# A two-layer hybrid backbone: MLP weights converted by HBM-to-HBM casting DMAs, and the RG-LRU gate loop split in two

## The chip, the cores and the metric

The kernel runs on all 8 cores of one Trainium2 chip. Every core computes one element of the batch with the same program and no exchange between cores. The metric is the device time in microseconds of the slowest core; a lower time is better.

## What is computed

x (8 x 2048 x 1024) and a context of 256 tokens go through two layers. Each layer is: RMSNorm and adaLN modulation, one input projection, three kinds of token mixers, one output projection, a gated residual, then a modulated squared-ReLU MLP (1024 to 4096 to 1024). The part on which the change works is the first kind of mixer, the RG-LRU, in both directions, and the weights of the MLP:

```python
r = jax.nn.sigmoid(gates[0])
i = jax.nn.sigmoid(gates[1])
log_a = -LRU_C * r * jax.nn.softplus(-lam)
a = jnp.exp(log_a)
b = jnp.sqrt(-jnp.expm1(2.0 * log_a)) * (i * xc)
a_cum, h = lax.associative_scan(_lin_combine, (a, b), axis=1)
...
def sq_relu_mlp(h, w1, w2):
    return jnp.square(jax.nn.relu(h @ w1)) @ w2
```

All inputs are float32. The kernel multiplies in bf16, so each weight is converted once or more on its way.

## The kernel before

The tokens of one core (256 of context, then 2048 latent, 2304 in all) lie in SBUF as X, channels on the partitions, float32. CHUNKS cuts the token axis into one chunk of 256 and four of 512. The kernel runs these stages in order: load_x (x through three staging buffers, transposed on TensorE); then per layer ada (48 blocks of ada_w, 512 KB each, through five staging buffers, cast to bf16 in turn by VectorE and ScalarE, one small product each), derive, the norm of all chunks into HT, two small projections (Wl with 16 columns, W24 with 120), the groups, and mlp; at the end final.

The groups of a layer are two RG-LRU groups of 128 channels (group_a), then six pair groups (group_pair: three of linear attention, three of mLSTM). Each group projects HT, gates, scans and adds its part of the output projection to X (finish_group).

group_a loads four weights by wload: a DMA on SP's queue into one of two float32 staging buffers (STG), then a cast on an engine, which is POOL when nothing is said (L408 to L423). Wo takes the place of Wx in SBUF. Then come the projection with Wx, the one with Wg and its gelu, the convolution, and the gate loop (L670 to L693): for each of two directions and each chunk, two products with 128x128 gate matrices, a Sigmoid, two Exp, a Sqrt and a second Sigmoid on ScalarE, two multiplies on VectorE; after the five chunks a scan on VectorE (L369) over all tokens.

The MLP's weights are converted in the background while the RG-LRU groups run. bg_setup makes a list of 64 jobs per layer (32 blocks of w1, 32 of w2); bg(n), called at many places of group_a, takes n of them: SP loads 512 KB of float32, POOL casts, and SP stores 256 KB of bf16 to the HBM scratch w1s or w2s, one job late (bg_flush). All 64 are done within the two RG-LRU groups. mlp then reads w1s and w2s: a first pass over the 256 context tokens (layer 0 only), then two passes over 1024 latent tokens. A pass loads each w1 block once and each w2 block once for every 512 tokens, through six buffers each (wload_cached).

There is no scheduler. The order on each engine is the order in which the code is written; Sched keeps, per engine, a list of instructions with the semaphores they wait for, worked out from which bytes of SBUF and PSUM each reads and writes. DMAs take one of 32 semaphores in turn. SP issues all DMAs, in order, so a DMA that waits for its buffer holds those behind it.

In the profile most activations have line L329 (act), VectorE's and POOL's multiplies L332 (tt), casts and copies L347 (cp), matrix products L358 (mmg), the second product of the MLP L984, DMA issues L142.

Of the kernel before, what the change touches and what calls it, by code (L numbers as in the profile page):

```python
# [12 lines left out]
ALU = mybir.AluOpType  # L13
# [43 lines left out]
class Sched:  # L57
    def __init__(self, nc, n_dma_sems=32):
# [6 lines left out]
        self.dma_next = 0  # L65
        self.cnt = {e: 0 for e in ENG}
# [63 lines left out]
    def dma(self, qe, out, in_, sb_reads=(), sb_writes=(), **kw):  # L130
        deps = self._deps(sb_reads, sb_writes)
        i = self.dma_next
        self.dma_next = (self.dma_next + 1) % len(self.dma_sems)
        if self.dma_cnt[i] > 0:
            k = ('dma', i)
            if deps.get(k, 0) < self.dma_cnt[i] * 16:
# [6 lines left out]
                           self.dma_sems[i], 16))  # L143
        self.ninst += 1
# [124 lines left out]
def build(n_layers=DEPTH, dbg=None):  # L269
# [160 lines left out]
    def wload_cached(out, src, scr, key):  # L430
# [6 lines left out]
        else:  # L437
            s.wait_tok('sync', stok[key])
# [25 lines left out]
    def bg(n):  # L464
        for _ in range(n):
# [12 lines left out]
            bg_pend.append((scr, bf, key))  # L478

# [144 lines left out]
    def group_a(l, a, HT, last):  # L624
# [5 lines left out]
        wload(Wx, win_d[l][:, a * 128:(a + 1) * 128].rearrange('(k p) f -> p k f', p=128))  # L630
        wload(Wg, win_d[l][:, 256 + a * 128:256 + (a + 1) * 128].rearrange('(k p) f -> p k f', p=128))
        wload(GW, gatew_d[l][:, a * 512:(a + 1) * 512].rearrange('p (i c) -> p i c', c=128))
# [10 lines left out]
        bg_alloc()  # L643
        bg(2)
        proj(HT, Wx, 128, lambda pb, t0, n, s_: (cp(XA[:, t0:t0 + n], pb), bg(1)))
        wload(Wo, wout_d[l][a * 128:(a + 1) * 128, :])
# [11 lines left out]
        proj(HT, Wg, 128, gelu_ev)  # L658
        o, _ = PC['convw']
# [7 lines left out]
        act(XCb, XCv, AF.Copy)  # L667
        T1A, T2A = T1, T2
        bg(2)
        for d in range(2):  # L670
# [4 lines left out]
            for ic, (t0, n, s_) in enumerate(CHUNKS):  # L675
                T1 = T1A if ic % 2 == 0 else T1b
# [5 lines left out]
                act(T1[:, 0:n], pr, AF.Sigmoid, bias=br)  # L682
                act(AB[:, t0:t0 + n], T1[:, 0:n], AF.Exp, scale=kap)
                act(T1[:, 0:n], T1[:, 0:n], AF.Exp, scale=kap2)
                act(T1[:, 0:n], T1[:, 0:n], AF.Sqrt, bias=EPSC[:, 1:2], scale=-1.0)
                act(T2[:, 0:n], pi, AF.Sigmoid, bias=bi)
                tt(T1[:, 0:n], T1[:, 0:n], T2[:, 0:n], ALU.mult)
                tt(BBf[:, t0:t0 + n], T1[:, 0:n], XCv[:, t0:t0 + n], ALU.mult)
            if d == 0:
                scan(H, AB, BBf, 0.0)  # L690
            else:
                scan(H2[:, 0:TC][:, ::-1], AB[:, 0:TC][:, ::-1], BBf[:, 0:TC][:, ::-1], 0.0)
                scan(H2[:, TC:T][:, ::-1], AB[:, TC:T][:, ::-1], BBf[:, TC:T][:, ::-1], H2[:, 0:1])  # L693
        tt(H, H, H2, ALU.add)
# [11 lines left out]
    PLIM = int(dbg[0][1:]) if (dbg and dbg[0][0] == 'p') else 99  # L706
# [322 lines left out]
    load_x()  # L1029
    stage = dbg[0] if dbg else None  # L1030
# [3 lines left out]
    for l in range(n_layers):  # L1034
# [29 lines left out]
        wload(Wl, win_d[l][:, 2048:2064].rearrange('(k p) f -> p k f', p=128))  # L1064
# [72 lines left out]
```

How the kernel before makes its waits and increments, by code:

```python
                def body(eng):  # L156
                    for waits, fn, sem, inc in self.q[e]:
                        for k, v in waits:
                            eng.wait_ge(self._semof(k), v)
                        if fn is not None:
                            fn(eng).then_inc(sem, inc)
```

## Time and profile before

| what | us |
|---|---|
| median of 2 runs | 4301.64 |
| the runs | 4281.28 and 4322.01 |
| the profiled execution, its own time | 4276.27 |
| its span, from the first to the last instruction of the slowest core | 4274.7 |
| spans of the 8 cores | 4264.9 to 4274.7 |
| busy: TensorE products | 2543.2 (59%) |
| busy: VectorE | 2011.3 (47%) |
| busy: ScalarE | 1659.4 (39%), of it 156 table loads 200.1 |
| busy: POOL | 529.4 (12%) |
| DMA: bytes moved, mean rate | 332.47 MB, 78 GB/s |

The busy times say how much work an engine has over the whole span, not where the time goes: the stages have different limits. A table load (ACT_TABLE_LOAD) is an instruction of its own on ScalarE, put in by the compiler where the next function isn't in the table that is loaded. "DMA share" is the mean busy share of the core's 16 DMA engines. The trace covers one execution on the slowest core; its times start at that core's first instruction.

### The profile page before, as it was taken

The page shows a single profiled execution, that of the slowest core. Times are in us where ns is not written, and L with a number is a line of the kernel's source. Part 1 is how long each engine was busy: PE and PEld are TensorE (multiplying, and loading weights), DVE is VectorE, ACT ScalarE, POOL GpSimd, SP SyncE. Part 2 cuts the span into 40 slices and gives each one's busy share as a digit, 9 for nine tenths or more (in the row PEclk, how much of TensorE's full clock was granted, in tenths as well). Part 3 has the DMA queues.
Part 4 walks back from the last instruction along what each step waited for, and adds up shares of the span by engine and source line. Part 5 has one row for each costly group of instructions (what it writes and reads, how often), then busy time and mean ns, then how long its engine had stood idle before and what let it go on. Part 6 is the DMA issues. An engine that isn't in the chain of part 4 may idle for free.

```text
span 4274.7 us, 53337 instructions; the slowest of 8 cores (4264.9 to 4274.7 us)
## 1 busy us (share of the span) xinstructions
PE 2543.2 (59%) x14036; PEld 1251.9 (29%) x14036; DVE 2011.3 (47%) x4256; ACT 1659.4 (39%) x2970; POOL 529.4 (12%) x834
## 2 busy tenths in 40 slices
PE   3143246657565567998952331665555575698995
PEld 2110022323333235443421110232323233243443
DVE  4245366566565663404212463566566566531314
ACT  1464633433435343303115647324435345421302
POOL 0023301101123030000000331011113032100000
PEclk7565565666665658999975655665665656699996
DMA  7556510000000005242373663000100100024242
GB/s 198 138 142 191 179 25 12 15 25 17 17 13 16 18 16 158 79 141 67 119 207 94 185 208 124 16 26 1 30 18 11 28 12 22 15 89 133 62 134 110
DMA packets 333588, 332.47 MB, mean 78 GB/s; under 512 B 19760, under 2 KB 244208, under 8 KB 333296
## 3 DMA queue, kind: packets, MB, share of 16 engines
q1 hardware_dynamic: 333296, 329.06, 26.4%
q8 instruction: 124, 2.03, 0.2%
q14 instruction: 168, 1.38, 0.1%
HBM read 287.06 MB, written 41.94 MB: 77 GB/s over the span
## 4 chain that ended last, share of the span: by engine, by line
PE 45%; DVE 19%; ACT 18%; issue 11%; SPq 4%; DMA 2%; DVEq 1%; ACTq 0%; POOL 0%; POOLq 0%
PE psum L358 33%; ACT arena L329 14%; PE psum L984 11%; DVE arena L343 7%; DVE arena L332 7%; DVE arena L369 4%; SPq L142 4%; ACT L329 3%; PE psum L366 1%; DVE arena L347 1%; DVEq L159 1%; DMA arena<-ada_w 1%; DMA arena<-w2s 0%; ACT arena L1010 0%; DMA arena<-w_in 0%
## 5 line engine op out<-in xcount | busy, mean ns | idle before, releaser
L358 PE MATMUL psum<-arena 128*128 128x512 bf16 (+6 forms) x11028 | 1977.2, 333 | 1619.3 <-ACT arena L329 1232.3
L358 PEld LDWEIGHTS psum<-arena 128*128 128x128 bf16 (+3 forms) x11028 | 952.9, 110 | 2638.8 <-issue 2171.5
L329 ACT ACTIVATE arena<-arena 128x512 bf16<-128x512 f32 (+10 forms) x1759 | 941.3, 560 | 1202.7 <-DMA arena<-ada_w 302.1
L332 DVE TENSOR_TENSOR arena<-arena 128x512 bf16<-128x512 f32 (+7 forms) x696 | 425.6, 611 | 752.2 <-ACT arena L329 740.6
L329 ACT ACTIVATE arena<-psum 128x512 f32<-128x512 f32 (+6 forms) x724 | 337.8, 477 | 816.0 <-PE psum L358 773.8
L343 DVE SCALAR_TENSOR_TENSOR arena<-psum,arena 128x512 f32<-128x512 f32 (+1 forms) x648 | 409.6, 712 | 456.0 <-PE psum L984 456.0
L984 PE MATMUL psum<-arena 128*128 128x512 bf16 (+1 forms) x2304 | 476.1, 368 | 15.4 <-DVE arena L343 6.9
L347 POOL CAST arena<-arena 128x1024 bf16<-128x1024 f32 (+3 forms) x170 | 202.1, 1196 | 1805.5 <-PE psum L358 1416.9
L343 DVE SCALAR_TENSOR_TENSOR arena<-arena 128x128 bf16<-128x128 f32 (+9 forms) x484 | 291.5, 625 | 210.2 <-ACT arena L329 176.1
L332 DVE TENSOR_TENSOR arena<-psum,arena 128x256 bf16<-128x256 f32 (+4 forms) x848 | 298.5, 382 | 154.0 <-PE psum L358 139.5
L329 ACT ACTIVATE arena<-psum,arena 128x256 f32<-128x256 f32 (+1 forms) x299 | 187.1, 637 | 359.4 <-PE psum L358 339.2
L984 PEld LDWEIGHTS psum<-arena 128*128 128x128 bf16 x2304 | 224.7, 98 | 266.6 <-issue 27.1
L329 ACT ACT_TABLE_LOAD x156 | 200.1, 1283 | 71.7 <-PE psum L358 31.7
L332 POOL TENSOR_TENSOR arena<-arena 128x128 bf16<-128x128 bf16 (+1 forms) x420 | 174.4, 434 | 418.8 <-ACT arena L329 393.3
L369 DVE TENSOR_TENSOR_SCAN arena<-arena 128x128 f32<-128x128 bf16 (+2 forms) x444 | 201.0, 518 | 34.3 <-ACT arena L329 32.9
L347 DVE CAST arena<-psum 128x512 bf16<-128x512 f32 (+3 forms) x130 | 81.2, 636 | 244.4 <-PE psum L358 243.2
L343 DVE SCALAR_TENSOR_TENSOR arena<-arena,psum 128x128 f32<-128x128 f32 (+1 forms) x624 | 182.8, 321 | 14.7 <-ACT arena L329 13.0
L339 POOL TENSOR_SCALAR arena<-arena 128x128 bf16<-128x128 bf16 x204 | 101.0, 495 | 491.4 <-DVE arena L347 364.3
L347 DVE COPY arena<-psum 128x512 f32<-128x512 f32 (+5 forms) x140 | 63.7, 484 | 182.0 <-PE psum L366 156.6
L366 PE MATMUL psum<-arena 128*128 128x128 bf16 (+1 forms) x704 | 93.2, 280 | 82.5 <-DVE arena L347 52.9
L347 DVE CAST arena<-arena 128x1024 bf16<-128x1024 f32 (+3 forms) x65 | 36.9, 568 | 169.6 <-DMA arena<-ada_w 127.6
L366 PEld LDWEIGHTS psum<-arena 128*128 128x128 bf16 (+1 forms) x704 | 74.3, 137 | 102.9 <-issue 99.1
(12 smaller groups left out, 154.8 us busy)
## 6 DMA issues: line engine op xcount, KB each, us to landing
arena<-w2s SPq DMA_DIRECT2D x288, 256.0 KB, 2.7
arena<-mlp_w SPq DMA_DIRECT2D x128, 512.0 KB, 5.0
arena<-ada_w SPq DMA_DIRECT2D x96, 512.0 KB, 8.3
arena<-w1s SPq DMA_DIRECT2D x160, 256.0 KB, 2.7
arena<-w_in SPq DMA_DIRECT2D x56, 512.0 KB, 4.6
w1s<-arena SPq DMA_DIRECT2D x64, 256.0 KB, 2.9
w2s<-arena SPq DMA_DIRECT2D x64, 256.0 KB, 2.6
arena<-x SPq DMA_DIRECT2D x16, 512.0 KB, 4.4
```

Of the source, the lines that this page charges most:

```text
L142: self.q[qe].append((waits, (lambda eng, out=out, in_=in_, kw=kw: eng.dma_start(out=out, in_=in_, **kw)), self.dma_sems[i], 16))
L159: eng.wait_ge(self._semof(k), v)
L329: s.op(e, lambda en: en.activation(out=out, in_=in_, func=func, **kw), reads=R_(in_, bias, scale), writes=[out])
L332: s.op(e, lambda en: en.tensor_tensor(out=out, in0=in0, in1=in1, op=op), reads=[in0, in1], writes=[out])
L339: s.op(e, lambda en: en.tensor_scalar(out=out, in0=in0, scalar1=s1, scalar2=s2, op0=op0, op1=op1), reads=R_(in0, s1, s2), writes=[out])
L343: s.op('vector', lambda en: en.scalar_tensor_tensor(out=out, in0=in0, scalar=sc, in1=in1, op0=op0, op1=op1), reads=R_(in0, sc, in1), write ...
L347: s.op(e, lambda en: en.tensor_copy(out=out, in_=in_), reads=[in_], writes=[out])
L358: inst = en.matmul(out, lhsT=l, rhs=r, start=(i == 0), stop=(i == n - 1))
L366: s.op('tensor', lambda en: en.transpose(out, in_, ident), reads=[in_, ident], writes=[out])
L369: s.op('vector', lambda en: en.tensor_tensor_scan(out=out, data0=d0, data1=d1, initial=init, op0=ALU.mult, op1=ALU.add), reads=R_(d0, d1, ...
L984: en.matmul(pb, lhsT=w, rhs=r, start=st_, stop=sp_)),
```

## The change

1. convert_all(layers) converts the MLP's weights of a layer with ten DMAs issued by POOL, from the float32 inputs in HBM to the bf16 scratch in HBM: eight for w1 (each reads 128 rows of 4096 and writes pieces of 128 elements) and two for w2. Each has a semaphore of its own (dma_fresh) and waits for nothing. Layer 0's are placed behind load_x, layer 1's between the groups and the MLP of layer 0. Every w1 block then waits for all eight DMAs of w1.
2. The background jobs are gone: group_a no longer calls bg_alloc, so bg does nothing.
3. Wl and the four weights of group_a are cast on ScalarE, no longer on POOL.
4. The gate loop is split: first all Sigmoids of a direction, r into AB and i into BBf, then a second loop over the chunks with the rest. The Sqrt becomes Ln and Exp(0.5 x).
5. Places to stop for debugging (cut), without effect here.

```diff
+    def dma_fresh(self, qe, out, in_, **kw):
+        sem = self.nc.semaphore('s_f%d' % len(self.dma_sems)).__enter__()
+        self.dma_sems.append(sem)
+        self.dma_cnt.append(1)
+        i = len(self.dma_sems) - 1
+        tok = (('dma', i), 16)
+        self.q[qe].append(([], (lambda eng, out=out, in_=in_, kw=kw: eng.dma_start(out=out, in_=in_, **kw)), sem, 16))
         self.ninst += 1
         return tok
...
             dst = scr if len(out.shape) == 2 else scr.rearrange('p (k f) -> p k f', f=out.shape[2])
             stok[key] = s.dma('sync', dst, out, sb_reads=[out])
         else:
-            s.wait_tok('sync', stok[key])
+            tk_ = stok[key]
+            for t_ in (tk_ if isinstance(tk_, list) else [tk_]):
+                s.wait_tok('sync', t_)
             s.dma('sync', out, scr if len(out.shape) == 2 else scr.rearrange('p (k f) -> p k f', f=out.shape[2]),
                   sb_writes=[out])
...
+    def convert_all(layers):
+        for l in layers:
+            w1toks = []
+            for k in range(8):
+                w1toks.append(s.dma_fresh(
+                    'gpsimd', w1s_d[l][:, :, k * 128:(k + 1) * 128].rearrange('f p c -> p f c'),
+                    w1_d[l][k * 128:(k + 1) * 128, :].rearrange('p (f c) -> p f c', c=128)))
+            for f in range(32):
+                stok[('w1', l, f)] = w1toks
+            for g in range(2):
+                tk = s.dma_fresh('gpsimd', w2s_d[l, g * 16:(g + 1) * 16],
+                                 wm2_d[l][g * 2048:(g + 1) * 2048, :].rearrange('(f p) d -> f p d', p=128))
+                for f in range(g * 16, (g + 1) * 16):
+                    stok[('w2', l, f)] = tk
...
-        wload(Wx, win_d[l][:, a * 128:(a + 1) * 128].rearrange('(k p) f -> p k f', p=128))
-        wload(Wg, win_d[l][:, 256 + a * 128:256 + (a + 1) * 128].rearrange('(k p) f -> p k f', p=128))
-        wload(GW, gatew_d[l][:, a * 512:(a + 1) * 512].rearrange('p (i c) -> p i c', c=128))
+        wload(Wx, win_d[l][:, a * 128:(a + 1) * 128].rearrange('(k p) f -> p k f', p=128), e='scalar')
+        wload(Wg, win_d[l][:, 256 + a * 128:256 + (a + 1) * 128].rearrange('(k p) f -> p k f', p=128), e='scalar')
+        wload(GW, gatew_d[l][:, a * 512:(a + 1) * 512].rearrange('p (i c) -> p i c', c=128), e='scalar')
...
-        bg_alloc()
-        bg(2)
         proj(HT, Wx, 128, lambda pb, t0, n, s_: (cp(XA[:, t0:t0 + n], pb), bg(1)))
-        wload(Wo, wout_d[l][a * 128:(a + 1) * 128, :])
+        wload(Wo, wout_d[l][a * 128:(a + 1) * 128, :], e='scalar')
...
-            for ic, (t0, n, s_) in enumerate(CHUNKS):
-                T1 = T1A if ic % 2 == 0 else T1b
+            for (t0, n, s_) in CHUNKS:
                 bg(2)
                 pr = ps(pj_bank(), n)
                 mmg(pr, [(GW[:, d * 2 + 0, :], XCb[:, t0:t0 + n])])
                 pi = ps(pj_bank(), n)
                 mmg(pi, [(GW[:, d * 2 + 1, :], XCb[:, t0:t0 + n])])
-                act(T1[:, 0:n], pr, AF.Sigmoid, bias=br)
-                act(AB[:, t0:t0 + n], T1[:, 0:n], AF.Exp, scale=kap)
-                act(T1[:, 0:n], T1[:, 0:n], AF.Exp, scale=kap2)
-                act(T1[:, 0:n], T1[:, 0:n], AF.Sqrt, bias=EPSC[:, 1:2], scale=-1.0)
-                act(T2[:, 0:n], pi, AF.Sigmoid, bias=bi)
-                tt(T1[:, 0:n], T1[:, 0:n], T2[:, 0:n], ALU.mult)
+                act(AB[:, t0:t0 + n], pr, AF.Sigmoid, bias=br)
+                act(BBf[:, t0:t0 + n], pi, AF.Sigmoid, bias=bi)
+            for ic, (t0, n, s_) in enumerate(CHUNKS):
+                T1 = T1A if ic % 2 == 0 else T1b
+                act(T1[:, 0:n], AB[:, t0:t0 + n], AF.Exp, scale=kap2)
+                act(AB[:, t0:t0 + n], AB[:, t0:t0 + n], AF.Exp, scale=kap)
+                act(T1[:, 0:n], T1[:, 0:n], AF.Ln, bias=EPSC[:, 1:2], scale=-1.0)
+                act(T1[:, 0:n], T1[:, 0:n], AF.Exp, scale=0.5)
+                tt(T1[:, 0:n], T1[:, 0:n], BBf[:, t0:t0 + n], ALU.mult)
                 tt(BBf[:, t0:t0 + n], T1[:, 0:n], XCv[:, t0:t0 + n], ALU.mult)
...
     load_x()
+    convert_all([0])
...
-        wload(Wl, win_d[l][:, 2048:2064].rearrange('(k p) f -> p k f', p=128))
+        wload(Wl, win_d[l][:, 2048:2064].rearrange('(k p) f -> p k f', p=128), e='scalar')
         proj(HT, Wl, 16, lambda pb, t0, n, s_: cp(LRT[:, t0:t0 + n], pb))
...
+        if l + 1 < DEPTH:
+            convert_all([l + 1])
         mlp(l, last)
```

On ScalarE, the gate loop of the first RG-LRU group, first direction, before (128x2304 is the copy ahead of it; psum marks a Sigmoid, and arena alone an Exp or a Sqrt; table loads aren't listed):

```order
L329 ACTIVATE arena<-arena 128x2304
L329 ACTIVATE arena<-psum,arena 128x256
L329 ACTIVATE arena<-arena 128x256 x3
L329 ACTIVATE arena<-psum,arena 128x256
L329 ACTIVATE arena<-psum,arena 128x512
L329 ACTIVATE arena<-arena 128x512 x3
L329 ACTIVATE arena<-psum,arena 128x512 x2
L329 ACTIVATE arena<-arena 128x512 x3
L329 ACTIVATE arena<-psum,arena 128x512 x2
```

and now, both directions (the lines have moved by 11):

```order
L340 ACTIVATE arena<-arena 128x2304
L340 ACTIVATE arena<-psum,arena 128x256 x2
L340 ACTIVATE arena<-psum,arena 128x512 x8
L340 ACTIVATE arena<-arena 128x256 x4
L340 ACTIVATE arena<-arena 128x512 x16
L340 ACTIVATE arena<-psum,arena 128x256 x2
L340 ACTIVATE arena<-psum,arena 128x512 x8
L340 ACTIVATE arena<-arena 128x256 x4
L340 ACTIVATE arena<-arena 128x512 x16
L340 ACTIVATE arena<-arena 128x2304
```

Before, the Sigmoids of a chunk stood around its Exps and its Sqrt. Now the ten Sigmoids of a direction stand together, and behind them four activations per chunk instead of three.

On POOL, the start of the program, before (casts of Wl, Wx, Wg, gate weights and background jobs):

```order
L166 UNCONDITIONAL_BRANCH
L347 CAST arena<-arena 128x128
L347 CAST arena<-arena 128x1024 x2
L347 CAST arena<-arena 128x512
L347 CAST arena<-arena 128x1024 x43
L347 CAST arena<-arena 128x512
L347 CAST arena<-arena 128x1024 x26
L347 CAST arena<-arena 16x128 x2
```

and now:

```order
L177 UNCONDITIONAL_BRANCH
L154 DMA w1s<-mlp_w 128x32x128 x8
L154 DMA w2s<-mlp_w 128x16384 x2
L358 CAST arena<-arena 128x1024
L358 CAST arena<-arena 16x128 x2
L358 COPY arena<-arena 128x18x64 x2
L361 MEMSET arena 128x2304
```

The ten DMAs of layer 0 are POOL's first work; behind them comes at once the first cast of a pair group. Layer 1's ten stand behind POOL's last multiply of layer 0.

## Rows read from the trace of the kernel before

**Rows 1.** The chain that ended last, shares of the span by engine.
```profile
PE 45%; DVE 19%; ACT 18%; issue 11%; SPq 4%; DMA 2%; DVEq 1%; ACTq 0%; POOL 0%; POOLq 0%
```

**Rows 2.** Stages in order of time: length, busy time of each engine, clock, DMA share.
```profile
core 6: us, PE busy (x) PEld busy (x) DVE busy (x) ACT busy (x) POOL busy (x), PEclk, DMA share, GB/s
0.00:64.00 64.00, 27.32 (x144) 24.20 (x144) 38.80 (x184) 6.21 (x13) 0.20 (x4) 0.89 0.60 174
64.00:178.00 114.00, 18.76 (x392) 15.24 (x392) 20.03 (x41) 31.28 (x39) 0.00 (x0) 0.51 0.84 217
...
240.00:420.00 180.00, 60.70 (x204) 20.96 (x201) 90.86 (x111) 100.77 (x122) 57.99 (x44) 0.59 0.65 188
420.00:590.00 170.00, 52.07 (x149) 15.36 (x149) 83.34 (x105) 92.41 (x107) 37.70 (x31) 0.55 0.39 125
590.00:1613.00 1023.00, 613.65 (x3788) 317.44 (x3786) 623.82 (x1550) 423.14 (x899) 169.59 (x339) 0.62 0.07 17
1613.00:1676.00 63.00, 58.11 (x492) 47.82 (x493) 13.62 (x32) 16.53 (x40) 0.00 (x0) 0.97 0.81 243
1676.00:1933.00 257.00, 233.81 (x1065) 104.71 (x1063) 65.68 (x99) 60.32 (x100) 0.00 (x0) 0.95 0.35 105
...
2187.00:2282.00 95.00, 16.40 (x376) 13.86 (x376) 16.52 (x24) 24.31 (x24) 0.00 (x0) 0.50 0.96 254
```

**Rows 3.** Waits over the run: total us, times, longest.
```profile
ACT arena L329 <- DMA arena<-ada_w: 302.1, 48, 109.5
```

**Rows 4.** ScalarE's groups from 292 to 332 us, one gate loop.
```profile
L329 ACT ACT_TABLE_LOAD x15 | 19.2, 1283 | 0.8
L329 ACT ACTIVATE arena<-arena 128x512 f32<-128x512 f32 x12 | 8.7, 721 | 0.5
L329 ACT ACTIVATE arena<-psum,arena 128x512 f32<-128x512 f32 x8 | 5.2, 683 | 0.0
L329 ACT ACTIVATE arena<-arena 128x256 f32<-128x256 f32 x3 | 1.5, 508 | 0.1
L329 ACT ACTIVATE arena<-psum,arena 128x256 f32<-128x256 f32 x3 | 1.4, 473 | 3.2 <-DVE arena L332 2.3 <-PE psum L358 0.8
```

**Rows 5.** ScalarE in order of time: start, us, instruction; one chunk.
```profile
299.73 1.28 ACT L329 ACT_TABLE_LOAD   x1
...
302.63 1.28 ACT L329 ACT_TABLE_LOAD   x1
303.93 0.72 ACT L329 ACTIVATE arena<-arena 128x512 f32<-128x512 f32 x1
...
307.30 1.28 ACT L329 ACT_TABLE_LOAD   x1
```

**Rows 6.** ScalarE's table loads from 590 to 1613 us.
```profile
L329 ACT ACT_TABLE_LOAD x12 | 15.4, 1283 | 14.9 <-PE psum L358 14.7
```

**Rows 7.** All engines in order of time, 235 to 255 us.
```profile
235.31 0.29 POOL L347 CAST arena<-arena 128x128 bf16<-128x128 f32 x1 [234.61 <-PE psum L358]
...
236.21 6.21 PE L358 MATMUL psum<-arena 128*16 128x256 bf16 x32 [1.04 <-POOL arena L347]
...
237.63 6.25 ACT L329 ACTIVATE arena<-arena 128x512 bf16<-128x512 f32 x9 [0.95 <-DVE arena L343]
...
253.15 1.20 ACT L329 ACTIVATE arena<-psum 24x512 bf16<-24x512 f32 x2 [0.17 <-PE psum L358]
253.24 2.02 POOL L347 CAST arena<-arena 128x1024 bf16<-128x1024 f32 x2 [17.65 <-PE psum L358]
```

**Rows 8.** Loads of mlp_w by SP in layer 0.
```profile
L142 SPq DMA_DIRECT2D arena<-mlp_w x64: 327/379/582, 254.8 to 500.2; - x64
```

**Rows 9.** Order of time: SP's first w1s load, POOL in a pair group, POOL's last.
```profile
1502.73 5.68 SPq L142 DMA_DIRECT2D arena<-w1s  x6
...
617.82 2.36 POOL L347 COPY arena<-arena 128x1152 bf16<-128x1152 bf16 x2 [61.17 <-DVE arena L347]
...
1570.71 0.45 POOL L332 TENSOR_TENSOR arena<-arena 128x128 f32<-128x128 f32 x1 [0.60 <-DVE arena L343]
```

More of the change, by code:

```diff
@@ L65, in __init__ @@
         self.dma_next = 0
+        self.n_pool = n_dma_sems
         self.cnt = {e: 0 for e in ENG}
@@ L132, in dma @@
         i = self.dma_next
-        self.dma_next = (self.dma_next + 1) % len(self.dma_sems)
+        self.dma_next = (self.dma_next + 1) % self.n_pool
         if self.dma_cnt[i] > 0:
@@ L143, in dma @@
                            self.dma_sems[i], 16))
+        self.ninst += 1
+        return tok
+    def dma_fresh(self, qe, out, in_, **kw):
[5 more added lines that the diff above has]
+        self.q[qe].append(([], (lambda eng, out=out, in_=in_, kw=kw: eng.dma_start(out=out, in_=in_, **kw)), sem, 16))
         self.ninst += 1
@@ L642, in group_a @@
         T1b = alloc([1, 512], F32)[:, 0, :]
-        bg_alloc()
-        bg(2)
         proj(HT, Wx, 128, lambda pb, t0, n, s_: (cp(XA[:, t0:t0 + n], pb), bg(1)))
-        wload(Wo, wout_d[l][a * 128:(a + 1) * 128, :])
+        wload(Wo, wout_d[l][a * 128:(a + 1) * 128, :], e='scalar')
+        cut(1)
         ga_rr = [0]
@@ L658, in group_a @@
         proj(HT, Wg, 128, gelu_ev)
+        cut(2)
         o, _ = PC['convw']
@@ L667, in group_a @@
         act(XCb, XCv, AF.Copy)
+        cut(3)
         T1A, T2A = T1, T2
@@ L693, in group_a @@
                 scan(H2[:, TC:T][:, ::-1], AB[:, TC:T][:, ::-1], BBf[:, TC:T][:, ::-1], H2[:, 0:1])
+        cut(4)
         tt(H, H, H2, ALU.add)
@@ L705, in build @@
         pass
-    PLIM = int(dbg[0][1:]) if (dbg and dbg[0][0] == 'p') else 99
+    PLIM = int(dbg[0][1:]) if (dbg and dbg[0][0] in 'pq') else 99
     def cut(n):
@@ L1082, in build @@
             groups = [('p', int(dbg[2]), 0)]
+        if stage and stage[0] == 'q':
+            groups = [('a', 0)]
         try:
@@ L1091, in build @@
         A.top = mark_l
-        if stage and (stage.startswith('g') or stage[0] == 'p'):
+        if stage and (stage.startswith('g') or stage[0] in 'pq'):
             dump(X[:, int(dbg[2]), :], T)
             break
+        if l + 1 < DEPTH:
+            convert_all([l + 1])
         mlp(l, last)
```

## The prediction

> **What bounds the kernel now.** I read the chain of waits first [rows 1]: no engine holds the whole span, TensorE has 45% of it, VectorE 19%, ScalarE 18%. So a change is worth what it is worth in its own stage, and the second view is the table of stages [rows 2]. It shows four kinds of stage. From 64 to 178 us (adaLN weights of layer 0) and again from 2187 to 2282 us (layer 1) every engine is mostly idle and the DMA engines are 0.84 and 0.96 busy: these stages are bound by loads, and the waits say the same, with ScalarE kept waiting 302.1 us by ada_w over the run [rows 3]. From 240 to 590 us run the two RG-LRU groups of layer 0, with ScalarE busy 193 of 350 us. The MLP of layer 0 begins at 1613 with its pass over the context, 63 us long, at a DMA share of 0.81; the passes over the latent tokens behind it are TensorE's (234 of 257 us) and use a third of the DMA time. The pair groups in between are not touched.
>
> Third, inside the RG-LRU groups. One gate loop (one direction, 292 to 332 us) holds fifteen ACT_TABLE_LOADs, 19.2 us of ScalarE, beside 16.8 us of activations [rows 4]. The order of time shows why the loop lasts as long as ScalarE does: each chunk of 512 takes 7.57 us (299.73 to 307.30), load, two Exp, load, Sqrt, load, two Sigmoid, without a pause in between [rows 5]. There are eight such loops (2 layers, 2 groups, 2 directions).
>
> **The gate loop: a gain.** The new loop does the ten Sigmoids of a direction first and then, chunk by chunk, Exp, Exp, Ln, Exp. That should need one load before the Exps and one before the next direction's Sigmoids, if Exp and Ln sit in one table. The trace says they do: from 590 to 1613 us, where 60 chunks run an Exp and then a Ln, there are only 12 loads [rows 6]. So 13 of 15 loads go: 13 x 1.283 = 16.7 us per direction. Five activations come in (Sqrt becomes Ln and Exp): 4 x 0.721 + 0.508 = 3.4 us. The pauses of ScalarE around the loads, 0.8 us in fifteen, mostly go too, 0.7 us. That is 14.0 us per direction, on the path, since nothing in the loop is slower than ScalarE: it needs 4 x 0.721 = 2.9 us per chunk after the change, VectorE's two multiplies take under 2. Eight directions: 112 us. What comes next late is the scan, which already stands on the path and is unchanged. I take 112; the ends are 106 (no pause saved) and 120 (1 us per direction more, where VectorE's multiplies of one chunk no longer lie behind the next chunk's loads).
>
> The Trainium skill, ScalarE: Activation LUTs, section "What ACT_TABLE_LOAD costs", puts a switch at about 2.66 us, a load of 1283 ns and a drain of about 1380 ns behind it. By that rule 104 loads removed would be an estimated 277 us instead of 133. The row of the load agrees on 1.283 us, but it shows no drain: the load at 302.63 ends where the Sqrt begins at 303.93 [rows 5]. I go by the row.
>
> **Weights of group A cast on ScalarE: a loss.** Four casts of each group and Wl of each layer move from POOL to ScalarE. Most find ScalarE idle. Two do not.
> - Wl (the low-rank projection): today POOL casts it at 235.31, and TensorE then runs four fifths of that projection, 6.21 us, while ScalarE still norms the last chunk (237.63 + 6.25, so until 243.9) [rows 7]. On ScalarE the cast stands behind the norm, so the whole projection comes after it: 6.2 us and the cast itself, about 7 us, twice, 14 us.
> - Wx of the first group, cast at 253.24 today, stands behind ScalarE's last evacuations of the second projection, which run until 254.35 (1.1 us, twice) [rows 7], and Wo, one 128x1024 cast of 1.05 us, now stands ahead of the gelu evacuations, four times. Together 6 us.
> That is 20 us. Bounds: 10 (the VectorE copies hide part) and 25.
> In return POOL no longer casts 128 MLP blocks while VectorE works beside it: 0 to 10 us, I take 5.
>
> **The MLP weights: where the gain can go.** Before, 64 jobs per layer each load 512 KB, cast on POOL and store 256 KB, in a time in which the DMA engines have little else to do: the loads run from 254.8 to 500.2 us [rows 8]. That is hidden behind the group. After, ten DMAs per layer do it from HBM to HBM. For layer 0 they stand first in POOL's queue, with nothing to wait for, so they run at time 0 beside the x and ada_w loads, the stages that DMA binds. For layer 1 they stand behind POOL's last work of layer 0, which ends at 1571 us [rows 9], 42 us ahead of the context pass that DMA binds.
>
> How much DMA time is it? Per layer 33.6 MB are read, 16.8 MB written. For w1 the pieces are 512 B (read) and 256 B (written), like ada_w's 512 B on the read side: 254 GB/s at a share of 0.96 [rows 2] is 265 GB/s, so 63 us. For w2 the rows are long: 243 GB/s at 0.81 is 300 GB/s, so 56 us. Sum 119 us of all 16 engines, if a write costs nothing beyond its read. If the writes cost as in the old route, which moved read and written bytes separately, it is 0.65 x 180 + 0.39 x 170 = 183 us, with the few other loads of those stages in it [rows 2]. No row shows a casting or an HBM-to-HBM DMA, nor how fast POOL feeds one. The nearest pace is that of the stream it replaces, 245 us for a layer [rows 8]: a share of 119/245 = 0.49.
>
> At 0.49 beside what is there: x stage 0.60 + 0.49 = 1.09, so 9% of 64 = 6 us; ada stage 0.84 + 0.49 = 1.33, so 38 us; context pass 0.81 + 0.49 = 1.30, so 19 us. Sum 63 us. The latent passes (0.35) and everything up to 1500 us have room. Bounds: nothing is lost if the stream only uses what others leave (a share of 0.16 in the ada stage; it would then take some 740 us, still before its data are wanted, at 1502.7 us, when SP issues the first w1s load [rows 9]). At the most, with 183 us of work pushed as fast as the engines take it, the first 178 us, in which 64 x 0.40 + 114 x 0.16 = 44 us are free, grow by 139, and the context pass, sharing by halves, by its own 51: 190 us.
>
> **Sum.** -112 + 20 - 5 + 63 = -34 us, with the ends -120 + 10 - 10 + 0 = -120 and -106 + 25 + 190 = +109. The profiled execution took 4276.27 us with a span of 4274.7, so it would be 4242. That execution was a little quicker than both timed runs (4281.28 and 4322.01). Set on the median 4301.64 it is 4268; I say 4265.
>
> **The rivals.**
> - *The stream hides* (chance 0.26). POOL feeds it slowly enough to fit between the other loads. For it: from 590 to 1613 the DMA engines are 0.07 busy [rows 2]. Against it: nothing holds it back at time 0. Losses under 20 us: -97 + 10 = -87, about 4215.
> - *The stream swamps the loads* (0.20), the slower side. One mechanism: on every DMA engine small casting writes take turns with ada_w's packets and cost more than their reads, so x and ada_w wait for nearly the whole of layer 0's conversion. For it: shares of 0.60 and 0.84 leave 44 us. Against it: 183 us is the old route's price, two transfers. By the bound above +190 - 97 = +93, so 4395. It decides from the point at which conversions cost over 183 us on the path (2%).
>  The Trainium skill, DMA: Bandwidth & Descriptors, section "Specifications", asks for at least 512 B per transfer, since below it the DMA engine reads, modifies and writes. The written pieces of w1 are 256 B, so this rule speaks for this rival; the trace has no HBM-to-HBM write to test it.
> - *POOL is held* (0.06). If feeding the DMAs keeps POOL busy past about 560 us, where the first pair group wants its copies (617.82 before [rows 9], some 58 us earlier with the gate loops shortened, plus the delay of the loads), all behind it waits. At 800 us that is some 240 us on top: about 4500.
> - *Loads stay* (0.03). If the placement of tables put Exp and Ln apart, each chunk would need two loads: ten more per direction, 103 us back, so 4370.
> My forecast has 0.45.
>
> **How the numbers follow.** A measurement of this kernel can tell about 2%, 86 us, from no change. Faster by more: most of half of the first rival and a tenth of the forecast, and the far ends of both, 0.27. Slower by more: over half of the second rival, the third, and a tail of the forecast, 0.20. Within: 0.53. The range 4180 to 4430 leaves out the quickest corner and POOL held.
>
> **What would show it.** In the changed profile: table loads 156 - 104 = 52; a gate loop of 24 to 25 us instead of 39; the projection after the norm 7 us later; a new DMA queue with some 50 MB per layer, finished before 500 us; ada_w landing slower, so that the first RG-LRU group starts near 285 instead of 240 us; the context pass at 80 us. I am wrong if the ada stage stays at 114 us or passes 190, if conversion is still running at 1500 us, or if POOL's first cast in a pair group waits for POOL itself.

## The result and the profile after

The changed kernel takes 4432.17 us (median of 11 runs, 4397.85 to 4514.21); the kernel before takes 4315.43 (10 runs, 4278.63 to 4441.78) beside it. The ratio is 1.0282, 95% interval 1.0218 to 1.0346: slower. The forecast, 4265, was wrong in its sign, and the outcome lies just outside its range; it is the rival in which the stream swamps the loads, at 4395. The medians above include runs that a disturbance of one die makes longer; the ratio and everything below compares undisturbed runs, 4398 us after with 4279 before, but for the traces of experiments 3 and 4, which are of disturbed runs and are read up to 400 us only, where TensorE's granted clock is that of the others (0.58 to 0.60 from 170 to 400 us). The change is +119 us; the rival's sum was +93, set on the median 4301.64, so that its 4395 comes nearer than its sum does.

The page of the changed kernel: engines, DMA queues, chain.

```profile
PE 2566.2 (58%) x14036; PEld 1262.8 (29%) x14036; DVE 1983.4 (45%) x4256; ACT 1542.5 (35%) x2916; POOL 371.9 (8%) x708
...
q1 hardware_dynamic: 239088, 228.38, 18.9%
q0 software_dynamic: 66368, 33.56, 7.8%
...
PE 44%; DVE 18%; ACT 15%; issue 10%; SPq 7%; DMA 4%; another core or an unknown queue 2%; DVEq 1%; ACTq 0%; POOL 0%; POOLq 0%
```

ScalarE and POOL both have less to do, and the chain of waits [rows 1] has moved from ScalarE (18 to 15%) to SP's queue and the DMAs (6 to 11%). q0 is the new queue. Its 7.8% of 4398.8 us is 343 us of all 16 engines, 172 per layer. Its 33.56 MB are the bytes written for both layers (16.8 MB each); what it reads, twice as much, is not in that number.

Stages of the changed kernel (start:end, length, busy times, TensorE clock, DMA share, GB/s):

```profile
0.00:64.00 64.00, 20.20 (x88) 17.21 (x88) 28.05 (x130) 6.21 (x13) 10.54 (x10) 0.84 1.07 158
64.00:205.00 141.00, 15.64 (x128) 12.99 (x128) 15.44 (x61) 4.23 (x4) 4.39 (x4) 0.53 1.10 144
205.00:310.00 105.00, 13.60 (x312) 11.54 (x312) 13.18 (x19) 21.49 (x21) 0.00 (x0) 0.50 0.90 210
310.00:470.00 160.00, 57.48 (x219) 24.04 (x216) 65.63 (x98) 92.06 (x155) 0.00 (x0) 0.64 0.07 20
1755.00:1871.00 116.00, 28.52 (x188) 19.69 (x185) 8.62 (x16) 5.88 (x9) 0.00 (x0) 0.62 0.95 141
```

Against [rows 2]: until 205 us the DMA engines are full (1.07 and 1.10, where a mean over engines and overlapping packets can exceed 1). The GB/s, 144 to 158 against 174 to 217, look like less, but count the new queue by what it writes: with its 3.68 and 11.16 MB of these two stretches taken as read they are 215 and 223. What is left for x and ada_w is 6.40 MB in 64 us and 9.05 MB in 141 us, 100 and 64 GB/s. The RG-LRU groups behind them, whose share was 0.65, now leave the DMA engines idle at 0.07: the work has moved from a stage with room to one without. The same in the MLP of layer 0, whose context pass now runs from 1684 to 1858 us: in its second part, the last row, the share is 0.95 and TensorE is idle three quarters of the time. TensorE's granted clock there is 0.62, where it was 0.97 [rows 2], and the products of the whole pass take 75.7 us instead of 58.1; how much of the loss is that, no run separates from the waits.

The balance, by the same instructions of VectorE in both traces (span 4274.7 before, 4398.8 after; the groups of a layer begin behind its adaLN weights, with the norm and the small projections):

| stretch | after minus before, us |
|---|---|
| x and adaLN weights, layer 0 (ends 169.7, now 310.3) | +140.6 |
| RG-LRU groups, layer 0 | -64.9 |
| pair groups | -5.3 |
| MLP of layer 0 | +110.6 |
| adaLN weights, layer 1 | +5.2 |
| RG-LRU groups, layer 1 | -65.9 |
| the rest of layer 1 | +3.8 |
| sum | +124.1 |

The new queue runs from 6 to 229 us and from 1645 to 1855 us, so no conversion is under way in the adaLN of layer 1 (2360 to 2469 us), and its +5.2 are not the conversions'.

One gate loop of the changed kernel, ScalarE in order of time (start, us, instruction):

```profile
440.27 2.12 ACT L340 ACTIVATE arena<-arena 128x2304 bf16<-128x2304 f32 x1 [7.45 <-DVE arena L354]
443.11 5.46 ACT L340 ACTIVATE arena<-psum,arena 128x256 f32<-128x256 f32 x10 [0.72 <-PE psum L369]
448.59 1.28 ACT L340 ACT_TABLE_LOAD   x1
449.89 13.05 ACT L340 ACTIVATE arena<-arena 128x256 f32<-128x256 f32 x20
469.67 1.28 ACT L340 ACT_TABLE_LOAD   x1 [6.73 <-DVE arena L380]
```

Ten Sigmoids, one load, twenty activations at a mean of 0.65 us, without a pause [rows 4, 5]. From the bf16 copy to the scan it was 40.1 us and is 22.2 (-17.8); from that scan to the next direction's, 43.3 and now 27.7 (-15.6). Eight directions: -134.

Now the loads. POOL from time 0, ScalarE in the adaLN stage, and SP and TensorE in the context pass, all of the changed kernel:

```profile
1.58 5.33 POOL L154 DMA_DIRECT2D w1s<-mlp_w  x3 [0.89 <-POOLq L281]
29.45 1.68 POOL L154 DMA_DIRECT2D w1s<-mlp_w  x1 [22.54 <-issue]
...
98.37 1.68 POOL L154 DMA_DIRECT2D w1s<-mlp_w  x1 [19.26 <-issue]
100.04 1.06 POOL L154 DMA_DIRECT2D w2s<-mlp_w  x2
```

```profile
225.45 1.06 ACT L340 ACTIVATE arena<-arena 128x1024 bf16<-128x1024 f32 x1 [83.41 <-DMA arena<-ada_w]
```

```profile
1685.45 43.46 SPq L143 DMA_DIRECT2D arena<-w1s  x26
1729.01 126.50 SPq L143 DMA_DIRECT2D arena<-w2s  x32
```

```profile
1817.41 1.86 PE L1016 MATMUL psum<-arena 128*128 128x256 bf16 x8 [36.84 <-DMA arena<-w2s]
1850.90 7.59 PE L1016 MATMUL psum<-arena 128*128 128x256 bf16 x56 [31.62 <-DMA arena<-w2s]
```

POOL issues three DMAs at once, then each further one as an older one finishes (the first three land at 29.1, 42.4 and 60.9 us, the next three are issued 0.3 us after each): its queue holds only so much. It is free at 101 us, long before anything waits for it. ScalarE then waits 83 us for one ada_w block, and TensorE 37 and 32 us for w2s blocks of 256 KB, far more than sharing bandwidth by halves gives. The packets of the new queue explain them. In 1780 to 1870 us:

```profile
q0 software_dynamic: 267, 7.70, 74.6%
q1 hardware_dynamic: 1973, 3.59, 13.9%
```

7.70 MB in 267 packets is 29 KB per packet. w2 is two contiguous stretches, and its DMAs are cut into 32 KB pieces, 256 in all, 16 per engine. They run from 138 to 229 us and from 1773 to 1855, so that a new piece follows on each engine every 5 to 6 us, and each takes 4.6 us. The five w2s loads issued from 1767 to 1781 us land 75 to 83 us after their issue, where those issued before 1765 us took 7 to 10. My reading was that an engine finishes a piece before it turns to SP's descriptors, a turn of some 5 us. The trace alone doesn't show how they take turns, so the experiments had to test the length of a piece apart from the sum of the work.

### The profile page after: what moved, and what is told of

The parts are those of the page before. It is cut to its first block, busy times and chain, and to the rows that moved or that the text cites. A ratio compares the mean times of both kernels' runs of the same rounds, so it can differ in the third digit from the quotient of the medians.

```text
span 4398.8 us, 52054 instructions; the slowest of 8 cores (4385.8 to 4398.8 us)
## 1 busy us (share of the span) xinstructions
PE 2566.2 (58%) x14036; PEld 1262.8 (29%) x14036; DVE 1983.4 (45%) x4256; ACT 1542.5 (35%) x2916; POOL 371.9 (8%) x708
## 3 DMA queue, kind: packets, MB, share of 16 engines
q0 software_dynamic: 66368, 33.56, 7.8%
## 4 chain that ended last, share of the span: by engine, by line
PE 44%; DVE 18%; ACT 15%; issue 10%; SPq 7%; DMA 4%; another core or an unknown queue 2%; DVEq 1%; ACTq 0%; POOL 0%; POOLq 0%
PE psum L369 33%; ACT arena L340 14%; PE psum L1016 10%; SPq L143 6%; DVE arena L354 6%; DVE arena L343 6%; DVE arena L380 4%; DMA arena<-x 1%; DMA arena<-w1s 1%; DVE arena L358 1%; PE psum L377 1%; DMA arena<-w2s 1%; DVEq L170 1%; ACT L340 1%
## 5 line engine op out<-in xcount | busy, mean ns | idle before, releaser
L340 ACT ACTIVATE arena<-arena 128x512 f32<-128x512 f32 (+10 forms) x1817 | 971.9, 563 | 1418.3 <-DMA arena<-ada_w 442.0
L343 DVE TENSOR_TENSOR arena<-arena 128x512 bf16<-128x512 f32 (+7 forms) x696 | 413.6, 594 | 647.6 <-ACT arena L340 637.3
L354 DVE SCALAR_TENSOR_TENSOR arena<-arena 128x128 bf16<-128x128 f32 (+9 forms) x484 | 279.9, 600 | 211.5 <-ACT arena L340 177.6
L358 POOL CAST arena<-arena 128x1024 bf16<-128x1024 f32 (+1 forms) x24 | 15.5, 659 | 1943.6 <-DVE arena L343 1596.3
```

The lines of the kernel that those rows point to most:

```text
L340: s.op(e, lambda en: en.activation(out=out, in_=in_, func=func, **kw), reads=R_(in_, bias, scale), writes=[out])
L343: s.op(e, lambda en: en.tensor_tensor(out=out, in0=in0, in1=in1, op=op), reads=[in0, in1], writes=[out])
L354: s.op('vector', lambda en: en.scalar_tensor_tensor(out=out, in0=in0, scalar=sc, in1=in1, op0=op0, op1=op1), reads=R_(in0, sc, in1), write ...
L358: s.op(e, lambda en: en.tensor_copy(out=out, in_=in_), reads=[in_], writes=[out])
```

## Experiments

Ratios are to the kernel before, with 95% intervals. The expectations name some kernels by labels: e5_late_1k is experiment 4, e6_groups_pool experiment 5, e7_groups_act experiment 6 and e12_behind_wo experiment 11.

**1. The gate loop alone.** The kernel before with only the split loop; background jobs and POOL's casts stay.

```diff
-                act(T1[:, 0:n], pr, AF.Sigmoid, bias=br)
...
+                act(AB[:, t0:t0 + n], pr, AF.Sigmoid, bias=br)
+                act(BBf[:, t0:t0 + n], pi, AF.Sigmoid, bias=bi)
+            for ic, (t0, n, s_) in enumerate(CHUNKS):
...
```

> The kernel before with the split gate loop alone; background jobs, casts on POOL and everything else as before. Theory: the loop's gain stands by itself and all the loss of the changed kernel comes from the conversion DMAs. In the two traces a first direction (from the end of the bf16 copy to the scan) went from 40.1 to 22.2 us and a second (scan to scan) from 43.3 to 27.7 us, so 33.4 us per group, 134 us for four: 0.969 of before. Rival: a part of that gain came from the background jobs being gone (VectorE and POOL beside each other); then the loop alone gives the 112 us of the forecast or less, 0.974 or above.

Measured 4189 to 4193 us, 0.9786 (0.9758 to 0.9815): -91 us. The scans of one group are again 27.7 to 28.3 us apart, so the loop gains its full 134; yet 42 are not seen. They are lost between the groups (against the kernel before, the stretch from the second scan of a layer to its third gains 2.5 us and loses 6.6, where the shorter loop in it should bring 17.8). TensorE and POOL of this run, at the second group of layer 0:

```profile
409.21 16.11 PE L358 MATMUL psum<-arena 128*128 128x256 bf16 x73 [18.53 <-POOL arena L347]
```

```profile
401.75 1.04 POOL L347 CAST arena<-arena 128x1024 bf16<-128x1024 f32 x1 [1.52 <-DMA arena<-mlp_w]
407.92 1.04 POOL L347 CAST arena<-arena 128x1024 bf16<-128x1024 f32 x1 [5.12 <-DMA arena<-w_in]
```

The 40 jobs of the first group take longer than the shortened group, and Wx's cast stands behind them: 18.5 us of TensorE's time. Over the run TensorE waits 50.0 us for POOL's casts here, 5.8 in the kernel before. The jobs were free only while ScalarE was slow. So taking them away is worth more than the 5 us I gave it, once the loop is split.

**2. w2 in pieces of 1 KB.** The changed kernel; each w2 DMA gets an innermost stretch of 512 elements, engines and bytes as before.

```diff
-                tk = s.dma_fresh('gpsimd', w2s_d[l, g * 16:(g + 1) * 16],
-                                 wm2_d[l][g * 2048:(g + 1) * 2048, :].rearrange('(f p) d -> f p d', p=128))
+            w2o = w2s_d[l].rearrange('f p c -> (f p c)').rearrange('(n b e) -> b n e', b=2, e=512)
+            w2i = wm2_d[l].rearrange('f d -> (f d)').rearrange('(n b e) -> b n e', b=2, e=512)
...
+                w2toks.append(s.dma_fresh('gpsimd', w2o[g], w2i[g]))
```

> The changed kernel, with w2 converted in pieces of 512 elements (1 KB written) in place of 16384 (32 KB written), same bytes, same place in POOL's queue. Theory A (length of a turn): a hardware-queue load waits for one long piece at each of its turns, so the 83 us hole in the ada stage and the waits of 36.8 and 31.6 us in the context pass go; the whole is 60 to 100 us quicker than the changed kernel. Theory B (sum of work): the DMA engines are saturated either way, only the order changes; the whole stays within 20 us of the changed kernel, and short pieces may cost more than long ones.

Measured 4351 to 4365 us, 1.0171 (1.0141 to 1.0201), 47 us less, between the two forecasts. The two places answer differently. The adaLN stage ends at 308.3 us, not 310.3, though no ada_w block is held for 83 us any more. The longest waits of ScalarE there:

```profile
198.31 1.06 ACT L340 ACTIVATE arena<-arena 128x1024 bf16<-128x1024 f32 x1 [26.39 <-DMA arena<-ada_w]
225.12 1.06 ACT L340 ACTIVATE arena<-arena 128x1024 bf16<-128x1024 f32 x1 [25.75 <-DMA arena<-ada_w]
```

There only the sum of the work counts. The MLP of layer 0 gains 55 us; TensorE's waits for w2s, after and in this run:

```profile
PE psum L1016 <- DMA arena<-w2s: 84.4, 12, 36.8
```

```profile
PE psum L1018 <- DMA arena<-w2s: 29.1, 22, 5.7
```

The longest falls from 36.8 to 5.7 us (the third number). The loads beside w2 in the context pass (from 1756 us on) now land 12.4 us after their issue, in the median. Both theories hold, each in one place. Where a stage only streams, a load held for 80 us is made up by those behind it; where 256 KB blocks with six buffers feed TensorE, each hold is lost time.

**3 and 4. The conversions moved behind the stages that wait for loads.** Layer 0's behind its adaLN, layer 1's behind the context pass; in experiment 4 with the 1 KB pieces too.

```diff
-    convert_all([0])
...
         if l == 0:
+            s.wait_tok('gpsimd', ('vector', s.cnt['vector']))
+            convert_all([0])
         derive(l)
```

> The changed kernel with the same ten DMAs per layer, each set issued later: layer 0's after the last adaLN product, layer 1's after the context pass. Theory: the loss was where they stood, 141 us in the first two stages and 112 us in the context pass; both go, and nothing is lost in the RG-LRU groups or the latent passes: 4399 - 253 = about 4145, 0.965 to 0.97 of before. Rival (length of a turn): the 32 KB pieces of w2 hold the few loads of the RG-LRU groups and the w1s loads of the latent passes by some 35 to 80 us each time a load is needed within the 140 us of w2, so 50 to 150 us come back.

> Late placement and short pieces of w2 together. If the length of a turn matters it is quicker than the late placement alone by what that one loses to held loads (50 us or more) and lies at 0.965 or below; if only the sum of work matters both are the same within 15 us.

Measured 4280 to 4301 us, 1.0014 (0.9997 to 1.0032), and 4181 to 4192 us, 0.977 (0.9742 to 0.9798). Experiment 3 is as its rival said, 135 us above the 4145; experiment 4 gains on it by more than 50 us but misses its 0.965. The place is worth 2.7% and the pieces, once moved, another 2.4%: more than in place, since now the weights of the first RG-LRU group are what the long pieces hold. In experiment 3 the first scan comes at 392.5 us, in 4 at 328.2. Waits of ScalarE in experiment 3:

```profile
ACT arena L340 <- DMA arena<-gatew: 50.6, 4, 44.1
ACT arena L340 <- DMA arena<-w_out: 34.1, 1, 34.1
```

ScalarE waits 44 us for 256 KB of gate weights beside 32 KB pieces; in experiment 4 the same wait is 12.6 us.

**5 to 8. The conversions in portions in layer 0's groups.** All have the split loop and no background jobs. Experiment 5: a third of a layer (four of w1, four of w1, two of w2) at the end of the second RG-LRU group and of five pair groups, 1 KB pieces, casts on POOL. Experiment 6: the same, casts on ScalarE. Experiment 7: casts on ScalarE, w1 where the change has it, w2 at the ends of pair groups. Experiment 8: experiment 5 with 32 KB pieces.

```diff
+    conv_slots = {(0, 'a1'): [(0, range(4))], (0, 0): [(0, range(4, 8))], (0, 1): [(0, None)],
+                  (0, 2): [(1, range(4))], (0, 3): [(1, range(4, 8))], (0, 4): [(1, None)]}
```

> Split gate loop, no background jobs, the five kinds of casts back on POOL, and the conversions of both layers issued in six portions of 2 to 4 DMAs at the ends of groups of layer 0 (before: DMA share 0.07 from 590 to 1613 us), w2 in 1 KB pieces. Theory: a conversion costs 172 us of the DMA engines per layer and costs time only where loads are waited for; here they are not, so what is left is the loops' 134 us and some 9 us per layer from VectorE without POOL beside it: 0.965 of before. Rival: the loads of w_in that the pair groups wait for are held up by each portion, 10 us and more for each of six: 0.98.

> As e6_groups_pool, with the casts of Wl and of group A's weights on ScalarE as in the changed kernel. Theory: the projection with Wl then stands behind the norm, 10.2 us later per layer in the traces, and the Wo cast delays the gelu a little: 15 to 25 us slower than e6_groups_pool, so about 0.970. Rival: the casts cost nothing that counts: the same within 5 us.

> As e7_groups_act, but w1 of each layer is converted where the changed kernel does it (layer 0 at time 0, layer 1 behind POOL's last work of layer 0), only w2 is moved into the groups. This prices w1 by itself. Theory (sum of work): w1 is about half of the 172 us, so the first two stages grow by 88 less the 44 us that are free in them, and the context pass by 20 to 40: 65 to 85 us slower than e7_groups_act. Rival: the 256-byte writes are the main cost and w1 brings most of the changed kernel's 141 us at the start: over 130 us slower.

> As e6_groups_pool, with w2 in its 32 KB pieces. Theory A (length of a turn): loads of the groups that fall into the two 90 to 140 us stretches of w2 are held some 35 to 80 us, so 40 to 150 us slower than e6_groups_pool. Theory B (sum of work): the same within 10 us, since the groups load little.

| experiment | us | ratio | interval |
|---|---|---|---|
| 5 | 4188 to 4196 and one of 4242 | 0.9752 | 0.9627 to 0.9877 |
| 6 | 4239 to 4242 | 0.9834 | 0.9715 to 0.9952 |
| 7 | 4297 to 4316 and one of 4357 | 1.0032 | 0.9968 to 1.0095 |
| 8 | 4217 to 4232 and one of 4245 | 0.9805 | 0.9704 to 0.9907 |

Experiment 5 is 77 us ahead of the kernel before at its fourth scan (468.1 against 545.2 us) and loses most of it again in the pair groups, which become up to 21 us longer each. What ScalarE waits for shows why: w_in in experiment 5, then in the kernel before:

```profile
ACT arena L340 <- DMA arena<-w_in: 189.8, 12, 50.6
```

```profile
ACT arena L329 <- DMA arena<-w_in: 113.1, 4, 30.5
```

The end of a group is just where the next one's weights are loaded. These waits are beside 1 KB pieces: short pieces don't make a 512 KB load free of the stream. A DMA share of 0.07 in a stage does not say that a transfer is free in it; the moment counts. Experiment 8, with 32 KB pieces, is 29 us behind experiment 5, less than the 40 to 150 of one theory and more than the 10 of the other, and the two intervals overlap.

Experiment 6 held a surprise: its adaLN stage ends at 191 us, not at 168, with the same code there. POOL's first work in its trace:

```profile
1.60 5.26 POOL L154 DMA_DIRECT2D w1s<-mlp_w  x3 [0.90 <-POOLq L281]
```

Without casts POOL has nothing ahead of that portion that waits, so DMAs written 400 us down the program go out at 1.6 us. Some 23 us of the 48 between experiments 5 and 6 are that, not the casts; the RG-LRU groups of the two layers are 12 and 10 us longer, and that is what the casts cost. In experiment 7 adaLN ends at 240 us and the MLP of layer 0 takes 36 us more than before: eight w1 DMAs alone cost half of what ten do in the first place and a third in the second, 107 us together. That is 60 us above experiment 6, near the 65 to 85 forecast and far from its rival's 130, but experiment 6 already pays those 23 us at the start.

**9 and 10. Casts on POOL.** Experiment 9 is experiment 4, experiment 10 the changed kernel, each with its five casts back on POOL.

```diff
-        wload(Wl, win_d[l][:, 2048:2064].rearrange('(k p) f -> p k f', p=128), e='scalar')
+        wload(Wl, win_d[l][:, 2048:2064].rearrange('(k p) f -> p k f', p=128))
```

> e5_late_1k with one edit more: Wl and the four weights of group_a are cast on POOL again, as before the change. Tells what the move of the casts to ScalarE costs at a place where the conversions are out of the prologue. Theory C (the casts cost what the trace shows): after Wl's load the whole 16-column projection comes 10.2 us later per layer (10.66 against 20.8 us from the end of the norm to the first group's projection), and Wo's cast stands ahead of the gelu; 20 to 30 us in all, so a ratio of 0.970 to 0.972, about 4165 us. Rival D (POOL's casts are held, since in layer 0 POOL issues ten conversion DMAs right after adaLN and is stopped by its full queue, so that Wl waits for it): POOL is free only some 70 to 100 us after the issue began, the first group starts that much later than in e5_late_1k, and the ratio is 0.99 or more.

> The changed kernel with its casts of Wl and of group_a's weights on POOL, nothing else altered. POOL has issued its ten DMAs by about 101 us there, long before Wl is cast at about 315 us, so nothing holds it. Theory C: the first group's projection comes 10 us sooner in each layer, together 20 to 30 us, so about 4405 us and a ratio of 1.022 where the changed kernel has 1.028. If the casts cost nothing, the ratio stays at 1.028.

Experiment 10: 4375 to 4378 us, 1.0227 (1.0202 to 1.0252). So the casts on ScalarE cost 23 us in the changed kernel, as forecast. Their largest part in its trace is the low-rank projection, all of it now behind the norm:

```profile
378.37 6.45 ACT L340 ACTIVATE arena<-arena 128x512 bf16<-128x512 f32 x10 [0.95 <-DVE arena L354]
...
384.54 17.76 PE L369 MATMUL psum<-arena 128*16 128x256 bf16 x78 [8.63 <-ACT arena L340]
```

Against [rows 7], from the norm's end to the first group's projection is 20.8 us, not 10.7.

Experiment 9: 4174 and 4183 us and one of 4224, 0.98 (0.9722 to 0.9879), no gain over experiment 4's 0.977. Both theories again: POOL is held by its full queue, and Wl's cast comes at 255.9 us instead of 234 (experiment 11),

```profile
254.33 1.56 POOL L154 DMA_DIRECT2D w2s<-mlp_w  x1 [8.68 <-issue]
255.89 0.30 POOL L358 CAST arena<-arena 128x128 bf16<-128x128 f32 x1
281.41 1.04 POOL L358 CAST arena<-arena 128x1024 bf16<-128x1024 f32 x1 [25.22 <-DMA arena<-w_in]
```

while in layer 1, with nothing ahead of them, the end of adaLN to the first scan takes 141.8 us instead of the changed kernel's 153.1. This is the rival "POOL is held" in small, at a place where POOL's next work is close: Wl's cast is 22 us late, and the first scan 17 us later than in experiment 4. Theory C's 4165 is missed for that, and rival D's 0.99 too. The same trace shows what is left of the stream with 1 KB pieces: the first of the two latent passes, beside which layer 1's conversion now runs (until 1846 us), takes 24 us longer than before at nearly the same granted clock (0.97 and 0.98), 19.5 of them waits for w2s. So "the latent passes have room" was not right either.

**11 and 12. Behind Wo's cast.** From there no load is wanted for some 110 us, as POOL's next cast shows. Each layer's conversions stand in its own RG-LRU groups: experiment 11 has the eight of w1 in the first and the two of w2 in the second, experiment 12 all ten in the first. 1 KB pieces, casts on POOL, which is what holds the DMAs back until then.

```diff
         wload(Wo, wout_d[l][a * 128:(a + 1) * 128, :])
+        conv_slot((l, 'a%d' % a))
```

> Loop split, no background jobs, casts on POOL. Each layer's conversions stand in its own RG-LRU groups, in POOL's queue right behind the cast of Wo: the eight of w1 in the first group, the two of w2 (1 KB pieces) in the second. From there no load is wanted for some 110 us (first group: Wo cast at 262 us, next weights loaded at 380 us; second: 392 and 475 us). Theory A (conversions cost only what they take from loads that are waited for): about 110 us of engine time for w1 and 65 us for w2 fit into these stretches, the groups end where those of e6_groups_pool end (75 us before the kernel before, in each layer), pair groups and MLP take their old time, so 4275 - 151 = 4124 us, with some contention 4120 to 4150, ratio 0.963 to 0.97. Rival B (the conversions cost their engine time wherever they are, by power, HBM or shared engines, not by waited-for loads): as e6_groups_pool or worse, ratio 0.975 or more.

> As e12_behind_wo, but all ten conversions of a layer stand behind Wo's cast in the first RG-LRU group, 172 us of engine time from about 262 us on, so that they are still running when the second group's weights are loaded at 380 us, and POOL may still be held by its queue. Theory A: those loads are held, by some 15 to 40 us per layer, ratio 0.97 to 0.985, above e12_behind_wo by 0.7 to 2%. Rival B: equal to e12_behind_wo, since the work is the same.

Experiment 11: 4129 to 4130 us and one of 4160, 0.9651 (0.9592 to 0.9711). Experiment 12: 4126 to 4133 us, 0.9638 (0.956 to 0.9716). Both beat both kernels, as theory A of experiment 11 said: 150 us under the one before, 270 under the changed one. POOL in experiment 11:

```profile
262.39 1.04 POOL L358 CAST arena<-arena 128x1024 bf16<-128x1024 f32 x1 [3.95 <-PE psum L369]
263.37 5.27 POOL L154 DMA_DIRECT2D w1s<-mlp_w  x3
...
329.26 1.68 POOL L154 DMA_DIRECT2D w1s<-mlp_w  x1 [9.29 <-issue]
380.93 2.03 POOL L358 CAST arena<-arena 128x1024 bf16<-128x1024 f32 x2 [49.99 <-PE psum L369]
...
392.88 3.12 POOL L154 DMA_DIRECT2D w2s<-mlp_w  x2
477.79 1.26 POOL L358 CAST arena<-arena 128x1024 bf16<-128x1024 f32 x2 [81.79 <-DVE arena L343]
```

Its casts wait for TensorE and VectorE as they should, never for the queue, and for a load 3 us at most. The first pair group starts 76 us sooner than before, that of layer 1 150 us sooner (2566.6 against 2716.2), and the adaLN and MLP stages have their old length. The expectation for experiment 12 failed. All ten DMAs had been issued by 340 us, so POOL was free at 380, but they had not finished: the queue runs until 432 us, beside the loads of the second group. From 380 to 432 us:

```profile
q0 software_dynamic: 4750, 4.83, 87.7%
q1 hardware_dynamic: 464, 1.32, 8.6%
```

So 46 of its 182 us of engine time are spent there, in 1 KB pieces of w2, and POOL waited 11.4 us for gate weights and 3.6 for Wo. That showed in no time: the group ends no later than in experiment 11, and spreading wasn't needed.

The two windows of experiment 11, 255 to 381 us (w1) and 390 to 475 (w2), give the engine time of the new queue almost by itself:

```profile
q0 software_dynamic: 32896, 8.39, 80.0%
```

```profile
q0 software_dynamic: 8224, 8.39, 94.3%
```

w1: 0.80 x 126 = 101 us. w2: 0.943 x 85 = 80 us. By the clock they were quicker, since packets overlap (a share over 1): w1 ran from 269 to 355 us, 86 us at a share of 1.17, w2 from 396 to 475, 78 us at 1.02.

```profile
q0 software_dynamic: 32896, 8.39, 117.2%
```

## Why the prediction was wrong

- **Gate loop, 112 us: right in kind, a little low.** 134, or 16.7 us per direction in place of 14.0. One more load went than I counted: the page has 44 table loads, not 52, so 14 per loop and not 13, 1.3 us. And the thirty activations took 5.46 + 13.05 = 18.5 us, where the prices of [rows 4] make 20.0, 1.5 us. "Loads stay" fell.
- **Casts on ScalarE, 20 us: right.** 23 by experiment 10, most of it Wl: 9 to 10 us per layer where I had 7.
- **POOL's work gone, 5 us: too low.** In experiment 10, without jobs and with the casts on POOL, the RG-LRU groups of both layers are 151 us shorter than before; 134 are the loop, which leaves 17, beyond the upper end of 10. I looked at POOL beside VectorE and not at what the jobs become when the loop around them gets shorter; experiment 1 shows that.
- **Conversions, 63 us: this step failed.** They cost 140.6 + 110.6 = 251 us, and both stages are back at their old length within 1 us where the conversions stand elsewhere (experiment 11). With the other terms, -134 + 23 - 17 + 251 = 123, that makes the 124 of the balance. Two numbers in it were wrong, and the smaller was the engine time: 119 forecast, 172 measured, near the 183 of the old route. A casting DMA costs an engine about what a load and a store did. The larger was the pace: with 172 in place of 119 the same sum gives an estimated 113 us (19 + 62 + 32), and the other 138 came from the pace. "The nearest pace is that of the stream it replaces" took 245 us from [rows 8], but that stream was paced by POOL's casts and by two buffers, and the new one by nothing except the length of its queue. The upper bound, pushed as fast as the engines take it, gave 139 us for the first stages and 141 came; as near as that it is by luck, since with the measured 172 it gives 128. The text had said "nothing holds it back at time 0" under a rival and then priced the forecast by a pace that needs something to hold it back.
- **The context pass, 19 us with an upper bound of 51: the bound itself failed.** It grew by 112. Sharing by halves has no length of a piece in it; the 32 KB pieces are 55 us of that by experiment 2. The other 56 are not taken apart; TensorE's lower clock is in them.
- **The stream swamps the loads: right in outcome and place, half right in cause.** For x and ada_w it is the sum of work. That small writes "cost more than their reads" explains part at most: w1, with 256 B written at a time, took 101 us against an estimate of 63, but w2 took 80 in 1 KB pieces and 74 in its 32 KB pieces (experiment 8) against 56. The rule of the Trainium skill, DMA: Bandwidth & Descriptors, section "Specifications", on transfers under 512 B points the right way. No run here tells it from the rest, since w1 is also read in shorter pieces. w1's excess over the estimate is 1.6 and w2's 1.4; by the clock, 86 and 78 us, it is 1.4 for both.
- **POOL held**: not in the changed kernel, where POOL is free at 101 us.

The gain was real and not small: without the placement, loop and lost jobs are worth 150 us (experiment 11). The change put 343 us of DMA work where it made the kernel wait 251 us.

## What to carry to other kernels

A transfer without a dependence starts when its queue reaches it, not where it stands in the program, and takes all the DMA time it can get (share 1.07 to 1.10 here); before adding one, find what will hold it back, and place it behind an instruction after which few loads are wanted for as long as it takes. To price it, use the pace that nothing throttles, and do not borrow the pace of a stream that buffers or casts held back. Where other loads feed a working engine beside it, cut it into small pieces.

## What was not expected of the hardware

- Contiguous DRAM to DRAM stretches went as packets of 32 KB written (4.6 us each), and engines waited 32 to 44 us for loads of 256 KB beside them; with 1 KB pieces the longest wait for w2s was 5.7 us and that for gate weights 12.6. Loads of 512 KB of w_in were still waited for up to 50.6 us (experiment 5), against 30.5 before.
- Pieces of 1 KB cost little engine time: q0 has 355 us of all engines in experiment 11 with 82240 packets (8.6% of 4128.7), 343 us in the changed kernel with 66368. In place (experiment 2, 8.0% of 4362.9) it is 349.
- POOL issued three of the w1 DMAs at once; each further issue waited 7 to 23 us for room, and POOL with it.
- The table load costs 1.283 us and no drain is seen behind it, where the Exp starts 0.02 us after the load ends, or ahead of it (0.8 us before fifteen loads, [rows 4]). The loop agrees: a gain of 16.7 us per direction, with 3.4 us of added activations and 1.5 of quicker ones, is 18.6 us for 14 loads, 1.3 each.
